# Sums of squares of q and k as two single-pass matmuls, with GpSimd making the low parts

## What is computed

```python
h = rms_norm(x, norm1_g) * (1 + scale1) + shift1
z = h @ w_in
q, k, v, ca, cg = jnp.split(z, ...)          # 512 columns each
q = rms_norm(q.reshape(B, L, 8, 64), q_norm_g)   # x * rsqrt(mean(x * x, over 64) + eps) * g
k = rms_norm(k.reshape(B, L, 8, 64), k_norm_g)
conv_out = conformer_conv(ca, cg, ...)       # GLU, 31 taps along the tokens, LayerNorm over 64, swish
attn_out = neighbourhood_attention(q, k, v, rpb)
```

## Time and profile before

| what | us |
|---|---|
| median of three runs | 3176.0 |
| the profiled execution | 3175.94 |
| its span | 3174.2 |
| TensorE busy | 3117.6 (98%) |
| VectorE busy | 2304.2 (73%) |
| ScalarE busy | 1907.7 (60%) |
| GpSimd busy | 187.8 (6%) |

### The profile page before, as it was taken

How to read it: one execution, slowest core, us unless ns; L and a number is a source line. 1 busy time by engine, 2 the same in 40 slices (tenths; PEclk the granted TensorE clock), 3 DMA queues, 4 the chain that set the end, 5 groups by cost and what they waited for, 6 DMA issues and landing times.

```text
span 3174.2 us, 49405 instructions
## 1 busy us (share of the span) xinstructions
PE 3117.6 (98%) x19002; PEld 2799.1 (88%) x19002; DVE 2304.2 (73%) x3555; ACT 1907.7 (60%) x3129; POOL 187.8 (6%) x191
## 2 busy tenths in 40 slices
PE   7999999998999999999999999999999999999998
PEld 5777766787999999999999999999999999999997
DVE  6789848458777767777777777777777776777775
ACT  6244478444666666656666666666666666665664
POOL 0000000001010101010101001010101010101000
PEclk9999999999999999999999999999999999999999
DMA  9321266437575747575766666675757574757562
GB/s 345 126 77 57 79 218 224 146 112 282 200 283 199 284 183 289 212 281 211 257 232 258 231 246 241 237 259 212 262 199 282 199 286 185 288 213 282 208 250 93
DMA packets 140941, 692.78 MB, mean 218 GB/s; under 512 B 11040, under 2 KB 48432, under 8 KB 116912
## 3 DMA queue, kind: packets, MB, share of 16 engines
q1 hardware_dynamic: 131680, 663.55, 56.1%
q0 software_dynamic: 8128, 25.17, 3.2%
q10 hardware_dynamic: 912, 1.00, 0.2%
HBM read 650.35 MB, written 39.34 MB: 217 GB/s over the span
## 4 chain that ended last, share of the span: by engine, by line
PE 76%; DVE 1%; DMA 0%; issue 0%; POOL 0%; ACT 0%; POOLq 0%; DVEq 0%
PE psG L1902 35%; PE psG L1904 16%; PE psY L1921 5%; PE psY L1924 5%; PE psY L1922 5%; PE psY L1923 5%; PE psY L1925 5%; DVE idxu L1362 0%; DVE affT L1365 0%; DVE vals L1359 0%; DMA xg<-xhat_d,iall 0%; PE psY L1840 0%; POOL out L1967 0%; DVE yp L2173 0%; DVE ye L2167 0%
## 5 line engine op out<-in xcount | busy, mean ns | idle before, releaser
L1902 PE MATMUL psG<-xe,w_gu_hi_part 128*128 128x384 f32 x5632 | 1617.2, 358 | 0.0
L1904 PE MATMUL psG<-xe,w_gu_lo_part 128*128 128x192 f32 x5632 | 1410.3, 250 | 0.0
L1904 PEld LDWEIGHTS psG<-xe,w_gu_lo_part 128*128 128x128 f32 x5632 | 1074.7, 191 | 13.1
L1902 PEld LDWEIGHTS psG<-xe,w_gu_hi_part 128*128 128x128 f32 x5632 | 1057.4, 188 | 13.8 <-DVE xe L2233 0.4
L2148 DVE TENSOR_TENSOR w_gu_lo_part<-raw_gu,w_gu_hi_part 128x1024 fp32r<-128x1024 f32 x704 | 859.9, 1223 | 119.3 <-ACT w_gu_hi_part L2026 119.3
L2026 ACT ACTIVATE w_gu_hi_part<-raw_gu 128x1024 fp32r<-128x1024 f32 x704 | 739.4, 1053 | 9.9 <-DMA raw_gu<-in_w_gu 9.9
L2054 ACT ACTIVATE low<-psG 128x384 f32<-128x384 f32 x352 | 172.8, 491 | 690.6 <-PE psG L1904 690.6
L2183 DVE TENSOR_TENSOR gu<-psG,low 128x384 f32<-128x384 f32 x352 | 195.9, 557 | 489.2 <-ACT low L2054 486.4
L2153 DVE TENSOR_TENSOR w_dn_lo_part<-raw_dn,w_dn_hi_part 128x1024 fp32r<-128x1024 f32 x352 | 431.0, 1224 | 1.6 <-ACT w_dn_hi_part L2037 1.3
L2037 ACT ACTIVATE w_dn_hi_part<-raw_dn 128x1024 fp32r<-128x1024 f32 x352 | 368.0, 1045 | 3.6 <-PE psY L1925 3.6
L1921 PE MATMUL psY<-w_dn_hi_part,hs 128*128 128x512 f32 x704 | 282.6, 401 | 0.0
(11 more groups left out here) (230 smaller groups left out, 3040.5 us busy)
## 6 DMA issues: line engine op xcount, KB each, us to landing
raw_gu<-in_w_gu SPq DMA_DIRECT2D x176, 2048.0 KB, 8.3
raw_dn<-in_w_down SPq DMA_DIRECT2D x176, 1024.0 KB, 9.3
shared<-in_ada_w SPq DMA_DIRECT2D x8, 2048.0 KB, 8.8
w_raw<-in_w_in SPq DMA_DIRECT2D x20, 512.0 KB, 5.3
bias<-in_bias SPq DMA_DIRECT2D x6, 1536.0 KB, 14.7
shared<-in_ada_pairs SPq DMA_DIRECT2D x4, 2048.0 KB, 16.5
qk_d<-shared SPq DMA_DIRECT2D x8, 768.0 KB, 3.8
qk<-qk_d SPq DMA_DIRECT2D x8, 768.0 KB, 7.3
```

The source lines that it names most:

```text
L1902: pe.matmul(bank[:, 0:2 * CAP], wh, xe[:, k, :, :].rearrange("p a b -> p (a b)"), start=(k == 0), stop=False, skip_group_check=True)
L1904: mm = pe.matmul(bank[:, 0:CAP], wl, xe[:, k, 0, :], start=False, stop=(k == KD - 1), skip_group_check=True)
```

## The change

Three things change.

1. For seven of the eight q and k tiles (all but the last, k3) a sum of squares is two single passes of type float32r instead of one float32 matmul. ScalarE squares each chunk twice out of PSUM, once rounded into `sq_hi` and once in full into `sqz`. GpSimd, which did not take part, subtracts the two into `sq_lo`. TensorE multiplies both by `ones_r`, a float32r copy of the matrix.
2. TensorE's side jobs of a step have six places: in the middle and at the end of each chunk. A list of counts says how many jobs stand at each.
3. `sq_lo` and `ones_r` lie where `bias_p` is loaded. The two transfers of `bias_p` are therefore issued at s = 20, behind the last sum of squares that reads them, ahead of the v windows.

```diff
@@ in_parts @@
-    per = -(-len(jobs[s]) // NCH)
-    if s == NZ - 1:
-
-        return [jobs[s][:1], jobs[s][1:], []]
-    return [jobs[s][per * n:per * (n + 1)] for n in range(NCH)]
+    todo = jobs[s]
+    if s >= NZ:
+        counts = [len(todo), 0, 0, 0, 0, 0]
+    elif s == NZ - 1:
+        counts = [0, 1, 1, 1, 0, 0]
+    elif todo and todo[0][0] == "ss":
+        counts = [0, 0, 1, 1, 2, 2]
+    elif len(todo) > NCH:
+        counts = [0, 1, 1, 1, 1, 2]
+    else:
+        counts = [0, 1, 0, 1, 0, 1]
+    return [todo[sum(counts[:i]):sum(counts[:i + 1])] for i in range(2 * NCH)]
@@ front, names and buffers @@
+    sq_ready, sq_lo_ready = sem("square_ready"), sem("square_lo")
+    def qk_before(j):
+        return sum(1 for kind, _ in Z_TILES[:j] if kind in "qk")
+    LAST_QK = Z_TILES.index(("k", 3))
+            sq_hi = sb(c0, "sq_hi", [P, TOKENS], F32R)
+            sq_lo = sb(c0, "sq_lo", [P, 2, TOKENS], F32R)
+        ones_r = sb(c, "ones_r", [P, P], F32R)
@@ SyncE @@
                     if s == LAST + 1:
+                        sp.wait_ge(side_done, index[("ss", LAST_QK - 1, NCH - 1)] + 1)
+                        for h in range(2):
+                            sp.dma_start(bias_p[:, h], A["bias"][h][:, :, 0:ROW_SETS[1][5]]).then_inc(bias_first, 16)
                         for j in range(2):
                             wait_store(sp, "v", Z_TILES.index(("v", j)))
...
                         for h in range(2):
-                            sp.dma_start(bias_p[:, h], A["bias"][h][:, :, 0:ROW_SETS[1][5]]).then_inc(bias_first, 16)
                             sp.dma_start(bias_s[:, h], A["bias"][h][:, :, ROW_SETS[1][5]:BIAS_COLS]).then_inc(bias_first, 16)
@@ TensorE, side(job) and the loop @@
                     elif kind == "ss":
-                        pe.wait_ge(z_act, sum(acts[:j + 1]))
-                        mm = pe.matmul(bank, ones64[:, :], sqz[:, j % 2, chunk(n)], start=True, stop=True)
+                        if j == LAST_QK:
+                            pe.wait_ge(z_act, sum(acts[:j + 1]))
+                            mm = pe.matmul(bank, ones64[:, :], sqz[:, j % 2, chunk(n)], start=True, stop=True)
+                        else:
+                            pe.wait_ge(sq_lo_ready, NCH * qk_before(j) + n + 1)
+                            pe.matmul(bank, ones_r[:, :], sq_hi[:, chunk(n)], start=True, stop=False)
+                            mm = pe.matmul(bank, ones_r[:, :], sq_lo[:, j % 2, chunk(n)], start=False, stop=True)
...
-                            for k in range(KD):
+                            for k in range(KD // 2):
+                                z_part(s, n, k)
+                        for job in todo[2 * n]:
+                            side(job)
+                        if s < NZ:
+                            for k in range(KD // 2, KD):
                                 mm = z_part(s, n, k)
...
-                        for job in todo[n]:
+                        for job in todo[2 * n + 1]:
                             side(job)
@@ ScalarE @@
                     elif kind in "qk":
-                        act.activation(sqz[:, s % 2, :], prods, ACT.Square)
+                        if s == LAST_QK:
+                            act.activation(sqz[:, s % 2, :], prods, ACT.Square)
+                        else:
+                            for n in range(NCH):
+                                square = psZ[:, 3 * (s % 2) + n, :]
+                                act.activation(sq_hi[:, chunk(n)], square, ACT.Square)
+                                act.activation(sqz[:, s % 2, chunk(n)], square, ACT.Square).then_inc(sq_ready, 1)
...
+                    if s == Z_TILES.index(("q", 0)):
+                        act.wait_ge(ada_row, MODS + ROWS)
+                        act.activation(ones_r[:, :], ones64[:, :], ACT.Copy)
@@ GpSimd @@
                 m.then_inc(pads_set, 1)
+                for j, (kind, _) in enumerate(Z_TILES):
+                    if kind in "qk" and j != LAST_QK:
+                        for n in range(NCH):
+                            pool.wait_ge(sq_ready, NCH * qk_before(j) + n + 1)
+                            pool.tensor_tensor(sq_lo[:, j % 2, chunk(n)], sqz[:, j % 2, chunk(n)],
+                                               sq_hi[:, chunk(n)].bitcast(F32), ALU.subtract).then_inc(sq_lo_ready, 1)
```

More of the change, by code:

```diff
@@ L309, in front @@
         cs = sb(c, "cs", [P, KD, P // CG])
+        with ExitStack() as c0:
+            sq_hi = sb(c0, "sq_hi", [P, TOKENS], F32R)
         ada_b2 = sb(c, "ada_b2", [P, MODS, GC])
@@ L841, in _ @@
                         if kind == "ss":
-                            before = sum(1 for k, _ in Z_TILES[:j] if k in "qk")
+                            before = qk_before(j)
                             if before:
```

## The result

The changed kernel takes 3181.3 us (median of 20 executions, 3179.3 to 3182.7), the kernel before in the same session 3175.9 us (20 executions, 3174.6 to 3177.6). The ratio is 1.0016, 95% interval 1.0009 to 1.0023: it is slower by 5 us. The forecast was 3170.8 with a range up to 3174.3; it was wrong. The profiled execution after took 3179.3 us, the least of the twenty, with a span of 3177.5, so its trace can explain 3.4 of the 5.4 us.

A forecast was written before the change was run, and what follows sets the result against it. TensorE, busy for 98% of the span, was taken to bound the kernel. From 3175.94 us, -9.0 (passes) + 1.8 (VectorE held up) + 2.1 (bias) = -5.1 gave 3170.8 us, range 3167.6 to 3174.3.

The forecast's parts named there:

- VectorE's room: Between w_lo(9) and step 14, VectorE was said to have 4.8 us to spare for GpSimd's holding.
- 290.3 us for w_lo(13), with no waiting: Start of w_lo(13) by VectorE's own work alone, counted from w_lo(9); it had to start by 295.1.
- 6c - 4.8: TensorE's wait for w_lo at step 14, from six subtractions on taps of steps 9 and 10: 1.8 us.
- c: What one GpSimd subtraction takes from VectorE: between 0 and 1.2 us, taken as 1.1.
- Nothing is late there either: Steps 14 and 15: 6.3 us of room up to w_lo(17), so no delay with c = 1.1.
- The six places instead of three add no pass: TensorE's side jobs in a projection step: more places were said to add no pass.
- The passes: TensorE's 21 changed sums of squares at 0.45 us a pair instead of 0.88: 9.0 us saved.
- The rival without holding: GpSimd does not hold VectorE (c below 0.8), so 1.8 us fall away: 3169.0 us; chance 0.25.
- the starved one: GpSimd gets no turn until VectorE's row of taps breaks, so sums come late: about 3207 us; chance 0.05.
- ScalarE's six squares: Six squares instead of one at a step's head: 2.1 us more, seven times, hidden by the step's rest.
- The bias load: Attention's start: VectorE's first step waits for the later bias_p loads, 2.1 us paid in full.
- The signs to look for: Among others: three taps of 2.9 us, a w_lo wait of about 1.8 us at step 14; wrong if in another step.

The follow-up runs named there:

- Experiment 6: The changed kernel with ScalarE's w_hi of the next step ahead of Silu in the four steps that have one: 3174.4 us.
- Experiment 1: The changed kernel without GpSimd's subtractions, TensorE's second pass reading sq_hi again: 3171.4 us.
- experiment 3: The kernel before with the side jobs dealt out to six places, float32 sums kept: 3177.3 us.
- experiment 5: The changed kernel with the third sum at the step's end, in steps that have only sums: 3178.3 us.
- experiment 10: The kernel of experiment 9 with the third sum back in the middle of the third chunk: 3172.3 us.
- experiment 8: The changed kernel with single passes for q0 and k0 only, bias_p loaded in its old place: 3174.4 us.
- experiment 2: The kernel before with six squares of 512 columns instead of one of 1536 for q0 to k2, the rounded ones unread: 3176.95 us.
- experiment 4: The kernel before with only the two bias_p loads moved behind the last k store: 3178.4 us.
- experiment 7: The changed kernel with single passes for six tiles (not q3, k3) and bias_p loaded in its old place: 3180.2 us.
- experiment 9: The changed kernel with three repairs: third sum at step's end, w_hi ahead of Silu, six tiles with bias_p in its old place: 3169.4 us.

## Why the prediction was wrong

**Where it failed: VectorE's room.** The prediction wrote "290.3 us for w_lo(13), with no waiting" and made the wait 6c - 4.8. It left out the 2.86 us that VectorE waited for w_hi ahead of w_lo(13), as slack which a busier VectorE would use up. It is none: w_hi stands in ScalarE's queue behind Silu, and Silu waits for VectorE's own last multiplication. When VectorE is late the wait moves with it, and it is 2.71 us after the change. With it the account is 6 x 0.93 - 4.8 + 2.7 = 3.5 us, and 3.3 were lost, more than half of it already at the start of step 13. That step's own w_lo(13) the prediction did not check: by its own numbers it would be done at 290.3 + 6.6 + 1.2 = 298.1, when step 13 starts at about 297.8 (302.99 less twelve times 0.43). The link itself is shown by the trace of the change (Silu waits 4.62 us for L1101, w_lo 2.71 for w_hi). Experiment 6 took it away and both waits with it, but it also moved w_hi ahead of Silu in step 7, so it doesn't test the link alone. Experiment 1 shows the other half: without the subtractions VectorE still waits for w_hi there, and TensorE doesn't wait for w_lo.

**The second failure is the same one in step 16.** "Nothing is late there either", from 6.3 us of room up to w_lo(17), looked only at w_lo (and six times 1.1 is 6.6, so its own sum gave 0.3 us). The same late Silu also stands ahead of the logarithms that free psS, and the third sum comes 2.7 us earlier in its step by the new places. "The six places instead of three add no pass" is right (experiment 3), but a job put earlier uses up room even where it costs nothing alone. That took 6.7 us, 1.4 of them because the clock fell behind the pause; it was in neither the sum nor the rivals. Experiments 5 (2.7 us of the wait, some 3 us of time) and 10 (2.3 of wait, 2.9 of time) show the place, the waits more surely than the times. Experiment 1, with no subtraction beside the taps, has a wait of 1.1 us there instead of 5.1, and experiment 6, with VectorE 5.5 us earlier at Silu, one of 2.2: they show that VectorE's lateness reaches the third sum.

**The passes.** 9.0 us expected, about 8.3 found: a pair costs 0.48 us and not 0.45, inside its bounds. The mechanism was right, by the trace of the change and by that of experiment 8.

**GpSimd and VectorE.** Holding is mutual: c is 0.93 us, the mean over the four blocks of taps (0.92 for 17.81 against 15.04), where 1.1 was taken, and the subtraction takes 1.27 alone (1.2) and 2.65 beside taps ("up to 3"). Three taps of a block take 2.8 us and the others 1.85, nearly the three of 2.9 that it said to look for. By the Trainium skill (SBUF — State Buffer, section Who interferes with whom), which treats the contended port as an exclusive lock, VectorE would lose GpSimd's whole instruction, 1.27 us; the trace has the contention, with 0.93 us about three quarters of that. The rival without holding falls by experiment 1, the starved one by GpSimd's timeline: three subtractions were through within some four taps, and TensorE never waited for sq_lo.

**ScalarE's six squares.** Called hidden, and experiment 2 shows it for six tiles, beside taps that GpSimd does not hold. The cost behind it was too high: the six take 2.9 us (338.44 to 341.30 on ScalarE in the change) and the single one 1.3 to 1.4, so they take 1.5 us more and not 2.1.

**The bias load.** 2.1 us expected, 1.5 in the profiled execution (landings of 4.7 to 5.9 instead of the median of 6.3), with VectorE waiting for the DMA as said. That the clock can fall at attention's start was not foreseen. Medians put the whole at 1.7 us (experiment 4) to 2.7 (experiment 7). The fall stands in the profiles of experiments 1, 4 and 5 and not in the profiled execution of the change, which is its fastest; that it makes the 2 us between that one and the median is likely and not shown.

**The signs to look for.** The wait for w_lo at step 14 came as told (1.2 us), with one at step 13 ahead of it, and "a wait for w_lo in another step" had been named as what would prove the forecast wrong.

## What to carry to other kernels

A wait in front of an instruction is room only if its releaser doesn't itself wait, through another engine's in-order queue, for the engine whose room is counted: follow the releaser one queue further before adding it up. On an engine that is 92% busy, an addition on a neighbour is safe only when each such chain has been counted, for buffers that come free as well as for data. Here the strongest single cure was to put the work that TensorE needs (w_hi) ahead of what nobody waits for soon (Silu) in the in-order queue: 3174.4 us instead of about 3181.7. It took all three repairs together to turn the loss of 5 us into a gain of 7.

## What the runs showed of the hardware

- GpSimd's subtraction of two SBUF tiles of 128x512 (1.27 us alone) takes 2.65 us beside VectorE's taps with two SBUF inputs, and adds 0.93 us to VectorE's work, all of it on the tap that runs beside it (2.8 us instead of 1.85). VectorE's taps follow one another without a gap, and GpSimd gets in all the same.
- After TensorE's pause of 5.3 us at 373 the granted clock was 0.50 from 378 to 380 us and full from about 381, at a price of 1.4 us. In experiment 5 it fell to 0.50 behind a pause of 2.4 us too, in experiments 6 and 10, with one of 2.2 and 2.3, the profile shows 1.00. At attention's start it fell to about half for several microseconds in three of the five profiles with the late load and in none with the early one. Which executions it hits was not settled. The spreads agree: 0.9 to 2.0 us for the kernels with bias_p early and either no pause in step 16 or one of 5.2 us (experiments 2, 3, 7, 8 and 9), and 3.4 to 5.1 us for those with the late load or with a pause of 2.3 us. The kernel before, timed 20 to 33 times, spreads over 2.0 to 3.0 us, so the number of executions is a part of it.
